# Early blocks of the small experts: scores in three passes of rounded parts instead of plain float32 products

## What is computed

```
q = (xt @ w_query).reshape(T, 8, 2, 128)
scores = einsum('thpc,hpnc->thpn', q, sub_keys)
top_s, top_i = top_k(scores, 16)
cand = top_s[:, :, 0, :, None] + top_s[:, :, 1, None, :]
best_s, best_pos = top_k(cand, 16);  idx = ...;  gate = softmax(best_s)
act = gelu(einsum('cd,ced->ce', x, expert_u[idx]))
y = einsum('ce,ced->cd', gate * act, expert_v[idx])
```

## Time and profile before

| | |
|---|---|
| median of 3 runs | 3182.62 us (3180.82 to 3183.95) |
| profiled execution | 3180.15 us, span 3178.4 us |
| mean granted TensorE clock | 0.962 |
| busy: TensorE, VectorE, ScalarE, GpSimd | 2935.0, 1970.3, 1066.6, 598.9 us |
| selection from the first early block, layer one and two | 1279.12 to 1357.24, 2337 to 2415 us |
| spread, layer one and two | 1357.24 to 1457.84 (100.60 us), 2415.2 to 2515.9 us (100.70 us) |
| early chunks (L2347), both layers | 1024 matmul records, 230.0 us busy |

### The profile page before, as it was taken

The page is one execution under the profiler, slowest core; times in us unless marked ns, Lnnn a source line. Parts: engine busy times, 40 slices in busy tenths (PEclk is TensorE's granted clock), DMA queues, the critical chain, the costliest instruction groups (busy, mean ns, idle before and its releaser), DMA issues. The chain is left out here.

```text
span 3178.4 us, 50113 instructions
## 1 busy us (share of the span) xinstructions
PE 2935.0 (92%) x19260; PEld 2473.7 (78%) x19260; DVE 1970.3 (62%) x3006; ACT 1066.6 (34%) x1574; POOL 598.9 (19%) x327
## 2 busy tenths in 40 slices
PE   8979997899899689998999999988999999999997
PEld 7968884554444677887899999977798879999996
DVE  5875533300000444987788888865479778888887
ACT  4522221100000352234444444434422444444443
POOL 0022300111111000000244444410000004444442
PEclk9989988899999899999999999989999999999999
DMA  7400014899999713413555555553242155555553
GB/s 217 158 5 1 1 60 166 350 419 419 420 419 404 255 39 101 169 57 113 185 185 185 185 186 188 188 195 123 90 147 93 60 186 190 188 189 186 185 185 139
DMA packets 186319, 574.30 MB, mean 181 GB/s; under 512 B 22067, under 2 KB 88115, under 8 KB 161217
## 3 DMA queue, kind: packets, MB, share of 16 engines
q1 hardware_dynamic: 182480, 568.10, 49.0%
q0 software_dynamic: 3696, 4.21, 0.4%
HBM read 613.13 MB, written 11.27 MB: 196 GB/s over the span
## 5 line engine op out<-in xcount | busy, mean ns | idle before, releaser
L2542 POOL TENSOR_TENSOR u_low<-u_raw,u_top 128x1024 fp32r<-128x1024 f32 x192 | 464.6, 2420 | 1632.4 <-ACT u_top L2451 1632.4
L2369 PE MATMUL psum<-v_top,hid 128*128 128x512 f32 x1888 | 622.5, 392 | 8.2 <-DVE hid L2649 8.2
L2369 PE MATMUL psum<-h_parts,u_top 128*128 128x256 f32 x3072 | 560.0, 283 | 4.6 <-DVE h_parts L2692 4.6
L2369 PEld LDWEIGHTS psum<-h_parts,u_top 128*128 128x128 f32 x3072 | 491.2, 191 | 20.2 <-DVE h_parts L2692 5.4
L2658 DVE TENSOR_TENSOR hid<-gelu,hid 128x256 fp32r<-128x256 f32 x192 | 481.4, 2507 | 6.6
L2369 PE MATMUL psum<-h_parts,u_low 128*128 128x256 f32 x1536 | 434.7, 283 | 0.0
L2369 PEld LDWEIGHTS psum<-v_top,hid 128*128 128x128 f32 x1888 | 357.1, 189 | 80.9 <-issue 10.1
L2369 PE MATMUL psum<-v_low,hid 128*128 128x512 f32 x944 | 371.0, 393 | 0.0
L1627 PE MATMUL psum<-piece_raw,tile_cols 128*64 128x256 f32 x2496 | 288.1, 381 | 17.9 <-DMA piece_raw<-w_up_dram 7.9
L2468 ACT ACTIVATE v_top<-v_raw 128x1024 fp32r<-128x1024 f32 x192 | 203.6, 1060 | 285.1 <-PE psum L2369 285.1
L2369 PEld LDWEIGHTS psum<-h_parts,u_low 128*128 128x128 f32 x1536 | 294.1, 191 | 0.0
(11 more groups left out here) (518 smaller groups left out, 4670.6 us busy)
## 6 DMA issues: line engine op xcount, KB each, us to landing
v_raw<-expert_v_dram SPq DMA_DIRECT2D x236, 512.0 KB, 3.3
u_raw<-expert_u_dram SPq DMA_DIRECT2D x192, 512.0 KB, 4.5
piece_raw<-w_gate_dram SPq DMA_DIRECT2D x78, 1024.0 KB
piece_raw<-w_up_dram SPq DMA_DIRECT2D x78, 1024.0 KB
piece_raw<-w_down_dram SPq DMA_DIRECT2D x78, 1024.0 KB
in_raw<-w_in_dram SPq DMA_DIRECT2D x48, 1024.0 KB, 5.3
all_gates<-expert_u_dram SPq DMA_DIRECT2D x64, 512.0 KB, 3.4
query_raw<-w_query_dram SPq DMA_DIRECT2D x16, 1024.0 KB, 6.5
```

The source lines that it names most:

```text
L2369: last = nc.tensor.matmul(out, r32(lhs[i]), r32(rhs[j]), start=start and n == 0, stop=stop and n == 2, skip_group_check=True)
L2542: nc.gpsimd.tensor_tensor(r32(low_u[:, k, :]), raw_u[:, k, :], top_u[:, k, :], ALU.subtract).then_inc(u_low_done, 1)
```

## The change

The scores of the early blocks take three passes of rounded parts too. ScalarE rounds x (`x_top`, four operations of 512 columns, behind the copy to `h_full`) and each block (`top_of_early`, 1024 columns): the first three before the second scores, each later one behind the gelu of three blocks before. GpSimd subtracts both in place (`x_low` lies on `h_full`, `early_low` on `raw_e`). TensorE waits for GpSimd's low parts instead of the load. `early_top` has three buffers. The upper region grows from 24 to 44 KB per partition, so that the early blocks must end before group 21 (before: 26). `EARLY_SHARE` becomes 12 and 13 blocks before the lists, seven blocks over groups 1 to 20; with it `exp_after` becomes 6 and 20.

```diff
+TOPS_E = 3
-    EARLY_SHARE = ((11, 11), (1, 26))
+    EARLY_SHARE = ((12, 13), (1, 21))
...
+        floats = RAW_E * D, KD * T, KD * T
+        over = [S["upper_at"] + 4 * sum(floats[:n]) for n in range(4)]
+        low_e, x_low, x_top, top_e = (nc.alloc_sbuf_tensor_at(f"{name}_{nc.next_id()}", shape, F32, offset=o) for name, shape, o in
+                                      zip(("early_low", "x_low", "x_top", "early_top"),
+                                          ([P, RAW_E, D], [P, KD, T], [P, KD, T], [P, TOPS_E, D]), over))
...
                 def early_chunk(e, c):
                     if c == 0:
-                        pe.wait_ge(early_in[e % RAW_E], 16 * (e // RAW_E + 1))
+                        pe.wait_ge(e_low_done, e + 1)
                         if e >= 2:
                             pe.wait_ge(early_out, e - 1)
-                    last = nc.tensor.matmul(PS[:, 4 + e % 2, 0:T], raw_e[:, e % RAW_E, c * P:(c + 1) * P], h_full[:, c, :],
-                                            start=(c == 0), stop=(c == KD - 1), skip_group_check=True)
+                    s = slice(c * P, (c + 1) * P)
+                    last = three_passes(PS[:, 4 + e % 2, 0:T], (top_e[:, e % TOPS_E, s], low_e[:, e % RAW_E, s]),
+                                        (x_top[:, c, :], x_low[:, c, :]), c == 0, c == KD - 1)
...
-                pe.wait_ge(h_full_done, 4)
+                pe.wait_ge(x_low_done, 4)
...
                 def gelu_early(e):
                     act.wait_ge(early_done, e + 1)
                     nc.scalar.activation(early[:, e, :], PS[:, 4 + e % 2, 0:T], ACT.Gelu).then_inc(early_out, 1)
+                    if e + TOPS_E < E:
+                        top_of_early(e + TOPS_E)
+
+                def top_of_early(e):
+                    act.wait_ge(early_in[e % RAW_E], 16 * (e // RAW_E + 1))
+                    if e >= TOPS_E:
+                        act.wait_ge(early_done, e - TOPS_E + 1)
+                    nc.scalar.activation(r32(top_e[:, e % TOPS_E, :]), raw_e[:, e % RAW_E, :], ACT.Copy).then_inc(e_top_done, 1)
...
-                    nc.scalar.activation(h_full[:, 2 * n:2 * n + 2, :], quarter(4 + n), ACT.Copy).then_inc(h_full_done, 1)
+                    nc.scalar.activation(h_full[:, 2 * n:2 * n + 2, :], quarter(4 + n), ACT.Copy)
+                    nc.scalar.activation(r32(x_top[:, 2 * n:2 * n + 2, :]), quarter(4 + n), ACT.Copy).then_inc(h_full_done, 1)
+                for e in range(TOPS_E):
+                    top_of_early(e)
...
             def _(pool):
+                for n in range(4):
+                    two = slice(2 * n, 2 * n + 2)
+                    pool.wait_ge(h_full_done, n + 1)
+                    nc.gpsimd.tensor_tensor(r32(x_low[:, two, :]), h_full[:, two, :], x_top[:, two, :],
+                                            ALU.subtract).then_inc(x_low_done, 1)
+                for e in range(E):
+                    pool.wait_ge(e_top_done, e + 1)
+                    nc.gpsimd.tensor_tensor(r32(low_e[:, e % RAW_E, :]), raw_e[:, e % RAW_E, :], top_e[:, e % TOPS_E, :],
+                                            ALU.subtract).then_inc(e_low_done, 1)
...
-            upper_floats = RAW_E * D + KD * T
+            upper_floats = (RAW_E + TOPS_E) * D + 2 * KD * T
+            S["upper_at"] = gates_at + 4 * (T * NKEYS - upper_floats)
```

More of the change, by code:

```diff
@@ L2207, in small_experts @@
     with phase(nc, "dve_step x_turned h_full_done scores_done scores_out exp_ready exp_done rows_done lists_t lists_out "
-                   "hot_done g_done g_out early_in0 early_in1 early_in2 early_in3 early_done early_out") as (
+                   "hot_done g_done g_out early_in0 early_in1 early_in2 early_in3 early_done early_out e_top_done "
+                   "e_low_done x_low_done") as (
             memory, dve_step, x_turned, h_full_done, scores_done, scores_out, exp_ready, exp_done, rows_done, lists_t,
-            lists_out, hot_done, g_done, g_out, early_in0, early_in1, early_in2, early_in3, early_done, early_out), \
+            lists_out, hot_done, g_done, g_out, early_in0, early_in1, early_in2, early_in3, early_done, early_out, e_top_done,
+            e_low_done, x_low_done), \
         phase(nc, "transposed h_top h_low u_in0 u_in1 v_in0 v_in1 v_in2 v_in3 ln_in u_top_done u_low_done v_top_done "
@@ L2947, in second_layer @@
             assert nc.sbuf_base == base
+            gates_at = -(-nc.sbuf_base // 32) * 32
             S["all_gates"] = sbuf(nc, peer, "all_gates", [P, T, NKEYS])
-            upper_floats = RAW_E * D + KD * T
+            upper_floats = (RAW_E + TOPS_E) * D + 2 * KD * T
+            S["upper_at"] = gates_at + 4 * (T * NKEYS - upper_floats)
             spare = carve(S["all_gates"])
```

## The result

| | before (same chip) | after |
|---|---|---|
| median of 4 runs | 3181.72 us (3180.06 to 3183.95) | 3240.35 us (3234.54 to 3243.03) |
| ratio | | 1.0181, 95% interval 1.0168 to 1.0194 |
| span of the profiled execution, clock | 3178.4 us, 0.962 | 3241.2 us, 0.952 |

The change makes the kernel 58.6 us slower. The forecast was 3230 us and slower.

What follows compares the result with a forecast made beforehand. VectorE and TensorE were taken to bound the kernel in turns; 2 x (29.4 lost in the selection - 5 gained in the spread) = 49 us on 3180.15 gave 3229, stated as 3230, range 3184 to 3268.

Steps and rivals of the forecast that it cites:

- TensorE's three passes and the start: Early blocks: 2.88 us each; TensorE starts at 1283.3 instead of 1279.1, hidden under VectorE's selection.
- Supply: Early blocks' rounded parts: ready about 4.3 us after block e, wanted 5.76 us after it; costed at nothing.
- The third rival: Early blocks: ScalarE and GpSimd in series bound the supply, 3.84 us a block; 3207 us, chance 0.06.
- Alternation in the selection, the term that decided: Selection: VectorE's pair work and GpSimd's low parts exclude each other and alternate, costing 29.4 us a layer.
- the walk: Selection, step by step: 6.8 us in the first stretches, then 13.0 and 9.6 us in the second stretch's halves.
- the second rival: VectorE against GpSimd: only float32 pairs collide, +7 us a layer; 3197 us, chance 0.08.
- the fourth: Selection: VectorE's searches pay too, so every low part stops it, 67.5 less 5 us a layer; 3307 us, chance 0.08.
- The first rival: Selection: no collision that counts, only the spread gains, -10 us a layer; 3162 us, chance 0.14.
- The spread: Spread of the gates: gain 10 us from TensorE's chunks, less 5 us for four low parts; net gain 5 a layer.
- a mask is 1.4 us early in three groups of four: Spread: this lead softens each 2.3 us collision, so TensorE loses about 1.3 us each, 5 us in all.
- 3194 at the least: Low end of the alternation forecast: exclusive work must still fit the selection, +3 to +7 us a layer.
- last gate masks of layer one near 1478: Profile after, end of layer one's spread: last gate masks near 1478 instead of 1458.

Runs made afterwards that it cites:

- run 1: The changed kernel with GpSimd subtracting 8 columns instead of 1024 in all 32 early blocks, TensorE reading top for low: 3165.94 us, ratio 0.9955.
- run 4: The kernel before plus one unused GpSimd subtraction of 1024 columns for each of blocks 0 to 27, the block as both inputs: 3214.62 us, 1.0105.
- run 5: The kernel before plus unused GpSimd subtractions for blocks 0 to 27, with two different tiles (the block and h_full) as inputs: 3222.31 us, 1.0137.

## Why the prediction was right, point by point

- **TensorE's three passes and the start: right.** Timeline of the changed kernel, TensorE's first pass and two gelus of ScalarE:

```profile
1285.19 0.55 PE L2378 MATMUL psum<-x_top,early_top 128*128 128x256 f32 x1 [3.81 <-POOL early_low L2565]
...
1350.46 0.38 ACT L2450 ACTIVATE early<-psum 128x256 f32<-128x256 f32 x1 [1.44 <-PE psum L2378]
...
1353.34 0.39 ACT L2450 ACTIVATE early<-psum 128x256 f32<-128x256 f32 x1 [1.23 <-PE psum L2378]
```

  A block takes 2.88 us. The selection began 2.1 us later than in before, so the start is 1283.1 against the forecast 1283.3. It stayed hidden, as run 1 shows (85.36 against 85.22 us).
- **Supply: right.** Behind the start TensorE waited 1.1 us in the whole selection for low parts (4.9 less 3.8), and run 4 loses time without any such chain. The third rival falls.
- **Alternation in the selection, the term that decided: right in place and size.** Forecast 6.8 us for the short stretches and 22.6 for the long ones; measured 6.8 (L2597, L2601) and 22.0 (the other four groups), five and four low parts in a row as walked through. By halves it is 13.0 against 13.6 and 9.6 against 8.4 us. Two small errors offset each other: a low part in the row costs 2.1 us and not 2.41, and ahead of the first row two low parts cost 3.1 us (L2616, L2621) where the walk had 1.0. bf16 pays as float32 does, which removes the second rival, and the searches pay nothing, which removes the fourth. The first rival is what run 1 built: 3165.94 against the 3162 it gave.
- **The spread: mis-sized.** Forecast a gain of 10 less 5, measured a loss of 0.7 and 0.6 us. Both terms were off.
  The gain from fewer and shorter chunks is 7.9 and 8.4 us (run 1). Here the sum itself had slipped: 1420.5 plus 25.8 to 28.8 ends at 1446.3 to 1449.3, not 1445.3 to 1448.3, and ten groups at the 12.15 us of four are 30.4, not 28.8. The rows used gave a gain of 7 to 11.5 us, and the measured one lies in it. In run 1 the last chunk ends 66.8 us behind the stage's start, where the sum had 63.3, and 25.9 us follow. Of these 3.5 us, 1.4 are the later first chunk: the 32 products ahead of it took 6.79 us at a granted clock of 0.52, in before 5.28 at 0.70. The two short waits for masks are 0.9.
  The collisions cost 8.6 and 9.0 us instead of 5. The timeline of the changed kernel has all four (layer one):

```profile
1406.82 3.40 DVE L2666 TENSOR_TENSOR hot_i<-constants,lists 128x1024 f32<-128x1024 f32 x1
...
1416.40 3.39 DVE L2668 TENSOR_TENSOR hot_j<-eighths,eighth_of 128x1024 f32<-128x1024 bf16 x1
...
1429.28 2.38 DVE L2659 TENSOR_TENSOR eighths<-constants,lists 128x512 bf16<-128x512 f32 x1 [0.50 <-PE psum L2372]
...
1439.85 2.93 DVE L2666 TENSOR_TENSOR hot_i<-constants,lists 128x1024 f32<-128x1024 f32 x1 [0.45 <-PE psum L2372]
```

Beside the 1.22 and 0.69 us of the earlier trace rows they are 2.2, 2.2, 1.7 and 1.7 us too long, 7.8 together. The forecast had 2.3 us for each, so VectorE's own cost was if anything too high; what failed is "a mask is 1.4 us early in three groups of four". That holds beside the plain products of before, and there run 4 loses nothing to three collisions and run 5 loses 2.1 of 5.7 us. In the changed kernel VectorE's waits for TensorE stay at 6.7 us, as short as the 6.2 of run 1, so nothing is taken up: VectorE is busy 7.7 us longer than in run 1 and the stage is 8.6 us longer. The first two collisions fall between VectorE's waits at 1395.97 and 1423.56, and TensorE waits 1.1 and 2.45 us for the masks behind them.

The profiled execution is 14 us above its forecast of 3229: 11.2 from the spread, less 2.0 in the selections (28.9 and 27.9 instead of 29.4 each), and 4.8 outside the four stages. That the median lies only 10 us above 3230 is in part the spread of the runs.

Two more slips of the prediction change nothing in the forecast. "3194 at the least" was worked out from +3 to +7 us a layer, which gives 3189 to 3197. And "last gate masks of layer one near 1478" leaves out the 5 us of collisions: its own sum gives 1482, and measured are 1489.5, of which 2.1 us had passed before the selection.

## What to carry to other kernels

In this kernel GpSimd's subtractions are free beside VectorE's searches and reductions. Where VectorE has a two-input operation or a cast waiting, each costs nearly its own length (2.1 of 2.4 us, 1.7 of 1.9); ask where it falls, not how much of it there is. Splitting it doesn't help, placing it does: 15 of 32 blocks, chosen by when their low part runs, took the loss of 1.8% to a gain of 0.4%. And slack that was read before a change belongs to the engine that sets the pace then; when the change shortens that engine's work, read the slack anew: three collisions in the spread cost nothing beside plain products (run 4), four cost 8.6 us beside the shorter ones.

## What the runs showed of the hardware that was not expected

- GpSimd's subtraction of 1024 float32 columns takes 1.89 us when both inputs are one tile and 2.40 us when they are two (runs 4 and 5).
- A pass of 256 columns followed the one before after 0.21 us instead of 0.12 in TensorE's first 5 us behind its idle 3.8 us. Windows of the changed kernel, granted clock 0.50 (the 1.2 GHz level) and then 1.00:

```profile
1285.19:1290.20 5.01, 5.01 (x23) 5.01 (x24) 4.94 (x29) 1.47 (x2) 4.51 (x2) 0.50 0.02 5
1290.40:1295.40 5.00, 5.00 (x44) 5.00 (x43) 5.00 (x27) 2.77 (x4) 2.41 (x2) 1.00 0.72 267
```

- In the spread, a group's 16 products took 3.67 us behind a wait of 2.45 us for a mask, against the 1.95 us of the earlier trace rows. The granted clock was 1.00 in the 7 us before the wait and 0.52 from 1419.84 to 1423.17. So waiting for VectorE can cost TensorE more than the wait; behind another wait, of 2.09 us at 1434.91, the products took 2.05 us. Timeline of the changed kernel:

```profile
1419.84 3.67 PE L2372 MATMUL psum<-hot_j,hot_i 128*128 128x128 f32 x16 [2.45 <-DVE hot_j L2668]
```
